# Both first products ahead of both transposes in the levels of a blockwise triangular inverse

## Chip, cores and metric

The kernel runs on one core of a Trainium2 chip. The metric is the device time of one execution in microseconds (us). The engines are called TensorE (PE in the profile), VectorE (DVE), ScalarE (ACT), GpSimd (POOL) and SyncE (SP).

## What is computed

A backbone of two layers over 512 latent tokens and 256 context tokens, 1024 channels wide, in float32. The change lies in layer 0, in the RWKV-7 part: 8 heads of 64 channels, each with a forward and a backward scan over the tokens.

```python
def update(S, w_t, k_t, v_t, a_t, b_t):
    sa = jnp.einsum('bhvk,bhk->bhv', S, a_t)
    return S * w_t[:, :, None, :] + sa[..., None] * b_t[:, :, None, :] + v_t[..., None] * k_t[:, :, None, :]
...
for d in range(2):
    rev = d == 1
    s_ctx, yc_d = rwkv_scan(state0, fc, d, need_ctx_out, rev)
    _, yl_d = rwkv_scan(s_ctx, fl, d, True, rev)
```

Attention, a gated convolution and two squared-ReLU MLPs make up the rest.

## The kernel before

The scan is done in 12 chunks of 64 tokens. Inside a chunk the effect of `sa` on later tokens is a unit lower triangular 64x64 system, which has to be inverted for every chunk, head and direction. The work goes over four pairs of heads (`for p in range(PAIRS)`, called pair 0 to 3 here). For each pair TensorE's program runs `chunk_matrices(p)` (the products of keys, decays and values), `inverse(p)` and `results(p)`.

`inverse(p)` refines an approximate inverse `X` in five levels, `lv` = 0 to 4, for two directions, `d` = 0 and 1, which do not depend on each other. One level of one direction is a ring over three engines:

- **First product** (`first_product`, L1011, 48 matmul records of 64x64): `LT` times `X`, into the two banks `2d` and `2d+1`. It waits for the sum of the level before (`x_ready`).
- **Mask** (`level_mask`, VectorE, L1379): the product, masked, to `W1` (`MT` in the profile).
- **Transposes** (`transposes`, L1024, 6 of 128x128): `X` of direction `d` to banks 4 and 5, three to each. Both directions use the same two banks, so the transposes of direction 1 wait, bank by bank, until ScalarE has copied those of direction 0 out (`xt_ready`).
- **Copies** (`inverse_rows`, ScalarE, L1250, one for each bank): to `XT`.
- **Second product** (`second_product`, L1038, in the last level L1041): needs the mask and both copies.
- **Sum** (`level_add`, VectorE, L1387): adds it to `X` (`xres` in the profile, since `X` and `LT` lie in that buffer). It releases the first product of the next level.

Other work of the neighbouring pairs is woven into TensorE's order by hand:

- `step(s)` (`state_step`, L1054): two per level, a product of the chunk-to-chunk recurrence of the pair before, of pairs 1 to 3 only. VectorE answers with two short instructions (L1395).
- `piece(i)` (`lora_piece`, L928): eight products for the decays and learning rates of the next pair, four in each of the levels 0 and 1, pairs 0 to 2 only. All go to bank 7, so piece `i` waits until ScalarE has taken the sigmoid of piece `i-1` out of it (`gate`, L1203).
- `bonus(p)` (L1085) in level 3.

ScalarE's and VectorE's orders are written out as well. In level 0 ScalarE does the copies of direction 0, loads a function table, does `gate` 0 and 1, then the copies of direction 1 and `gate` 2 and 3. In level 3 of the pairs 0 to 2 it does the copies of direction 0, a table load and two exponentials (L1209, L1211), and then the copies of direction 1. VectorE does mask 0, step, mask 1, sum 0, step, sum 1, with a scan (`cumulate`, L1311) in front of sum 0 in the levels 1 and 2 of the pairs 0 to 2, and another product (L1419) there in level 3. Meanwhile GpSimd multiplies and sums modulation weights (L890 to L896).

Of the kernel before, what the change touches and what calls it, by code (L numbers as in the profile page):

```python
# [61 lines left out]
def build(nc, A):  # L62
# [70 lines left out]
    def bank(i, lo=0, hi=512):  # L133
        return psum[i // 2][:, (i % 2) * 512 + lo:(i % 2) * 512 + hi]

    def K(name, lo=0, hi=None):
        a, n = cst_at[name]
        return cst[:, a + lo:a + (n if hi is None else hi)]
# [710 lines left out]
    def half(i):  # L849
        return slice(i * Q, (i + 1) * Q)  # L850

    def evacuated(p, i):

        kind = ORDER[i][0] in BY_ACT
        before = sum((k in BY_ACT) == kind for k, _ in ORDER[:i + 1])
        return (b_act, NACT * p + before) if kind else (b_dve, NDVE * p + before)
# [18 lines left out]
    with clear_then_block(S) as block:  # L875
# [44 lines left out]
        def _(pe):  # L920
# [82 lines left out]
            def first_product(p, lv, d):  # L1003

                pe.wait_ge(x_ready, 10 * p + 2 * lv + d + 1)
                if lv == 0:
                    pe.wait_ge(*evacuated(p, (18, 17)[d]))
                for g in range(GD):
                    for q in range(2):
                        for e in range(2):  # L1010
                            last = nc.tensor.matmul(bank(2 * d + e, g * Q, (g + 1) * Q)[half(q)], LT[half(e), d, g, q, :],  # L1011
                                                    X[half(e), d, g, q, :], start=True, stop=True)
                last.then_inc(s1_done, 1)

            def transposes(p, lv, d):

                n = 10 * p + 2 * lv + d
                for b in range(2):
                    if lv or d:
                        pe.wait_ge(xt_ready, 2 * (n - 1) + b + 1)  # L1020
                    else:
                        pe.wait_ge(*evacuated(p, 16))
                    for g in range(3 * b, 3 * b + 3):
                        last = nc.tensor.transpose(bank(4 + b, (g - 3 * b) * P, (g - 3 * b + 1) * P),  # L1024
                                                   X[:, d, g].rearrange("p q j -> p (q j)"), K("ident"))
                    last.then_inc(t_done, 1)
# [60 lines left out]
            def inverse(p):  # L1087

                def step(s):
                    if p:  # L1090
                        state_step(p - 1, s)

                def piece(i):
                    if p < PAIRS - 1:
                        lora_piece(p + 1, i)

                pe.wait_ge(*evacuated(p, 19))
                for lv in range(LVL):
                    first_product(p, lv, 0)
                    step(2 * lv + 1)  # L1100
                    transposes(p, lv, 0)
                    if lv < 2:
                        piece(4 * lv)
                    if lv == 3:
                        bonus(p)
                    first_product(p, lv, 1)
                    if lv < 2:
                        piece(4 * lv + 1)
                    transposes(p, lv, 1)
                    if lv < 2:  # L1110
                        piece(4 * lv + 2)
                    second_product(p, lv, 0)
                    step(2 * lv + 2)
                    if lv < 2:
                        piece(4 * lv + 3)
                    second_product(p, lv, 1)
# [941 lines left out]
```

## Time and profile before

| | us |
|---|---|
| three runs | 1876.32, 1867.37, 1876.82 |
| their median | 1876.32 |
| the profiled execution, its own time | 1864.56 |
| span of the profile in it | 1862.7 |
| TensorE busy | 1652.6 (89%) |
| the four inverses in the span | 435.7 to 707.1, in four parts |

The span is the time from the first to the last instruction in the profile. Lines in the profile are lines of the kernel before; a matmul row gives the instructions it merges and, in brackets, how long the engine stood still ahead of it and what ended that. "issue" means that no semaphore is seen to have ended it.

### The profile page before, as it was taken

The numbers are of one execution on the slowest core, as the hardware profiler recorded it, in microseconds if no ns is written. First come the engines' busy times: TensorE is split into PE (matmuls) and PEld (weight loads), VectorE is DVE, ScalarE is ACT, GpSimd is POOL, SyncE is SP. The second block draws the span as 40 slices with busy tenths as digits, with TensorE's granted clock in tenths as the row PEclk, the third lists the DMA queues.
The fourth block names the chain that finished last, engine by engine and source line by source line (L and its number), as shares of the span: only waits on it lengthen the run. The fifth ranks groups of instructions, "written<-read, shape, count | busy, mean of one in ns | idle before, by whom it ended". The sixth has DMA issues, their size and how long they took to land. (4 is left out here: it accounts for less than half of the span.)

```text
span 1862.7 us, 35286 instructions
## 1 busy us (share of the span) xinstructions
PE 1652.6 (89%) x15302; PEld 1294.3 (69%) x15302; DVE 799.7 (43%) x1083; ACT 578.4 (31%) x830; POOL 888.3 (48%) x352
## 2 busy tenths in 40 slices
PE   6699978958898887688999999989988799999995
PEld 2388847646777776364888888858867378888884
DVE  1421257666776763666211112680085821212125
ACT  2333235345353331414322223132221331323220
POOL 0443201039869580424778878843423434444442
PEclk9899989979999998798999999979999899999997
DMA  5341100003222131111443443311212112232221
GB/s 225 113 146 46 67 1 1 0 1 116 82 84 97 60 126 48 51 68 48 158 156 136 151 142 135 135 46 68 90 68 91 45 68 91 94 110 90 90 90 45
DMA packets 23449, 161.89 MB, mean 87 GB/s; under 512 B 2592, under 2 KB 3232, under 8 KB 4640
## 3 DMA queue, kind: packets, MB, share of 16 engines
q1 hardware_dynamic: 21744, 153.96, 23.3%
q10 hardware_dynamic: 1584, 6.13, 0.8%
q8 instruction: 100, 1.64, 0.4%
q14 instruction: 21, 0.17, 0.0%
HBM read 157.98 MB, written 2.10 MB: 86 GB/s over the span
## 5 line engine op out<-in xcount | busy, mean ns | idle before, releaser
L206 POOL TENSOR_TENSOR v<-raw,v 128x2048 fp32r<-128x2048 f32 x80 | 374.9, 4687 | 422.7 <-ACT v L195 348.6
L222 PE MATMUL bank<-hm,v 128*128 128x512 f32 x2304 | 538.8, 395 | 21.0 <-DVE hm L1758 10.0
L222 PEld LDWEIGHTS bank<-hm,v 128*128 128x128 f32 x2304 | 438.2, 191 | 122.3 <-issue 17.2
L222 PE MATMUL bank<-hid,v 128*128 128x512 f32 x1536 | 349.5, 389 | 0.0
L222 PEld LDWEIGHTS bank<-hid,v 128*128 128x128 f32 x1536 | 288.3, 188 | 59.9
L195 ACT ACTIVATE v<-raw 128x2048 fp32r<-128x2048 f32 x73 | 139.9, 1916 | 418.8 <-PE bank L222 418.8
L222 PE MATMUL bank<-h,w 128*128 128x512 f32 (+1 forms) x792 | 153.7, 357 | 14.2 <-POOL w L206 11.2
L1887 DVE TENSOR_TENSOR bank<-bank,rl 128x512 f32<-128x512 f32 x64 | 44.8, 700 | 275.9 <-ACT rl L1866 275.9
L222 PEld LDWEIGHTS bank<-h,w 128*128 128x128 f32 x792 | 129.8, 190 | 38.4 <-issue 13.4
L890 POOL TENSOR_TENSOR raw<-raw,cs 128x2048 f32<-128x2048 f32 x24 | 89.9, 3745 | 43.0 <-DVE at L1335 43.0
L1901 DVE TENSOR_TENSOR yb<-bank,yb 128x512 f32<-128x512 f32 x48 | 33.2, 692 | 170.8 <-PE bank L222 170.6
L894 POOL TENSOR_TENSOR raw<-raw 128x1024 f32<-128x1024 f32 (+1 forms) x48 | 95.9, 1998 | 3.8
L206 POOL TENSOR_TENSOR w<-raw,w 128x2048 fp32r<-128x2048 f32 x11 | 51.5, 4685 | 86.7 <-ACT w L195 86.7
L646 POOL TENSOR_TENSOR kk<-kk,knorm x32 | 12.4, 389 | 155.2 <-DVE knorm L785 155.2
L175 PE MATMUL bank<-cst 128*128 128x512 f32 x132 | 66.4, 651 | 7.7 <-PEq L1599 4.8
L1866 ACT ACTIVATE rl<-bank 128x512 f32<-128x512 f32 x64 | 37.6, 588 | 93.9 <-PE bank L222 74.1
L222 PE MATMUL bank<-ho,wo 128*128 128x512 f32 x192 | 50.1, 422 | 15.5 <-POOL ho L1566 11.0
L503 DVE TENSOR_TENSOR nb<-pad 128x770 f32<-128x770 f32 (+1 forms) x15 | 15.6, 1038 | 107.1 <-ACT pad L474 107.1
L206 POOL TENSOR_TENSOR wo<-raw,wo 128x2048 fp32r<-128x2048 f32 x4 | 19.4, 4849 | 83.9 <-ACT wo L195 83.9
L1585 DVE TENSOR_TENSOR ysq<-yb 128x512 f32<-128x512 f32 x28 | 45.4, 1622 | 32.3 <-ACT yb L1645 31.7
L1811 POOL TENSOR_TENSOR mprod<-mraw,cs 128x2048 f32<-128x2048 f32 x16 | 57.9, 3620 | 0.1
L222 PEld LDWEIGHTS bank<-ho,wo 128*128 128x128 f32 x192 | 38.7, 205 | 27.2 <-issue 13.0
(277 smaller groups left out, 2304.8 us busy)
## 6 DMA issues: line engine op xcount, KB each, us to landing
raw<-w_in SPq DMA_DIRECT2D x127, 1024.0 KB, 4.7
mraw<-wm_in SPq DMA_DIRECT2D x16, 1024.0 KB, 4.8
xres<-x_in ACTq DMA_DIRECT2D x1, 2048.0 KB, 9.3
xres<-x_in SPq DMA_DIRECT2D x1, 2048.0 KB, 9.1
out_T<-xres ACTq DMA_DIRECT2D x8, 256.0 KB, 2.0
kk<-ctx_in ACTq DMA_DIRECT2D x1, 1024.0 KB, 13.9
csa<-csa_in SPq DMA_DIRECT2D x1, 960.0 KB, 4.6
cst<-cst_in ACTq DMA_DIRECT2D x1, 864.0 KB, 17.3
```

The costliest lines, as they stand in the source:

```text
L175: nc.tensor.matmul(out[:, 0:width], K("ones"), cst[:, 0:width], start=True, stop=True)
L195: nc.scalar.activation(W[0][n % 2][:], raw[n % 2][:], ACT.Copy).then_inc(hi_ready[n % 2], 1)
L206: nc.gpsimd.tensor_tensor(W[1][n % 2][:], raw[n % 2][:], W[0][n % 2][:].bitcast(F32), SUB)\
L222: last = nc.tensor.matmul(bank(b(s, m), 0, hi - lo), W[w][s][:, k, m * P:(m + 1) * P], H[h][:, k, lo:hi], start=(k == 0 and w == h == 0), ...
L503: link(nc.vector.tensor_tensor(nb[:, a:N + 2], pad[j % 2][:, a:N + 2], pad[j % 2][:, a + 2:N + 4], ADD))
L890: nc.gpsimd.tensor_tensor(r[:], r[:], cs[:, :, 0].unsqueeze(2).to_broadcast([P, KT, 256]), MUL)\
L894: nc.gpsimd.tensor_tensor(r[:, 0:w, :], r[:, 0:w, :], r[:, w:2 * w, :], ADD).then_inc(mprod_ready, 1)
L1585: nc.vector.tensor_tensor(self.acc[:] if t == 0 else self.sq[:], y, y, MUL).then_inc(self.ready, 1)
L1811: nc.gpsimd.tensor_tensor(mprod[:], mraw[:], cs[:, :, 0].unsqueeze(2).to_broadcast([P, KT, 256]), MUL).then_inc(mprod_ready, 1)
L1866: nc.scalar.activation(rl[t % 2][:], bank(2 * (n % 2) + m), ACT.Relu)\
L1887: nc.vector.tensor_tensor(sq[t % 2], bank(2 * (n % 2) + m), rl[t % 2][:], MUL)\
L1901: i = nc.vector.tensor_tensor(yb[:, c, :], o, yb[:, c, :], ADD)
```

## The change

In each level TensorE now issues the first products of both directions ahead of the transposes of both. The pieces stay in their order, each behind a transposing group: piece 0 behind the first, 1 and 2 both behind the second. The lines of VectorE, ScalarE, GpSimd and SyncE are the same, and so is every instruction and every bank.

```diff
@@ -1098,16 +1098,15 @@
                 for lv in range(LVL):
                     first_product(p, lv, 0)
                     step(2 * lv + 1)
+                    first_product(p, lv, 1)
                     transposes(p, lv, 0)
                     if lv < 2:
                         piece(4 * lv)
                     if lv == 3:
                         bonus(p)
-                    first_product(p, lv, 1)
+                    transposes(p, lv, 1)
                     if lv < 2:
                         piece(4 * lv + 1)
-                    transposes(p, lv, 1)
-                    if lv < 2:
                         piece(4 * lv + 2)
                     second_product(p, lv, 0)
                     step(2 * lv + 2)
```

TensorE's program in pair 1, level 0, before. L1011 is a first product, L1054 a step, L1024 the transposes of one direction, L928 a piece, L1038 a second product; one listed instruction is two matmul records in the profile, where the operands are float32:

```order
L1011 MATMUL bank<-xres 64x64 x24
L1054 MATMUL bank<-kk 64x64 x4
L1024 MATMUL bank<-cst,xres 128x128 x6
L928 MATMUL bank<-lora,lw 128x256
L1011 MATMUL bank<-xres 64x64 x24
L928 MATMUL bank<-lora,lw 128x256
L1024 MATMUL bank<-cst,xres 128x128 x6
L928 MATMUL bank<-lora,lw 128x512
L1038 MATMUL bank<-MT,XT 64x64 x24
L1054 MATMUL bank<-Z,kk 64x64 x4
L928 MATMUL bank<-lora,lw 128x512
L1038 MATMUL bank<-MT,XT 64x64 x24
```

The same place after the change:

```order
L1011 MATMUL bank<-xres 64x64 x24
L1054 MATMUL bank<-kk 64x64 x4
L1011 MATMUL bank<-xres 64x64 x24
L1024 MATMUL bank<-cst,xres 128x128 x6
L928 MATMUL bank<-lora,lw 128x256
L1024 MATMUL bank<-cst,xres 128x128 x6
L928 MATMUL bank<-lora,lw 128x256
L928 MATMUL bank<-lora,lw 128x512
L1038 MATMUL bank<-MT,XT 64x64 x24
L1054 MATMUL bank<-Z,kk 64x64 x4
L928 MATMUL bank<-lora,lw 128x512
L1038 MATMUL bank<-MT,XT 64x64 x24
```

The first product of direction 1 has moved ahead of the first transposes; the second transposes now stand ahead of the second piece, so that the second and third piece are neighbours.

TensorE in pair 1, level 3, before, from its first product on:

```order
L1011 MATMUL bank<-xres 64x64 x24
L1054 MATMUL bank<-Z,kk 64x64 x4
L1024 MATMUL bank<-cst,xres 128x128 x6
L1085 MATMUL bank<-bs,cst 128x512
L1011 MATMUL bank<-xres 64x64 x24
L1024 MATMUL bank<-cst,xres 128x128 x6
L1038 MATMUL bank<-MT,XT 64x64 x24
L1054 MATMUL bank<-Z,kk 64x64 x4
L1038 MATMUL bank<-MT,XT 64x64 x24
```

And after the change:

```order
L1011 MATMUL bank<-xres 64x64 x24
L1054 MATMUL bank<-Z,kk 64x64 x4
L1011 MATMUL bank<-xres 64x64 x24
L1024 MATMUL bank<-cst,xres 128x128 x6
L1085 MATMUL bank<-bs,cst 128x512
L1024 MATMUL bank<-cst,xres 128x128 x6
L1038 MATMUL bank<-MT,XT 64x64 x24
L1054 MATMUL bank<-Z,kk 64x64 x4
L1038 MATMUL bank<-MT,XT 64x64 x24
```

Here the transposes of direction 0 stand behind the first product of direction 1. In the levels 2 and 4 nothing is left between the two groups of transposes, as the listing after the change shows with twelve in a row:

```order
L1011 MATMUL bank<-xres 64x64 x24
L1054 MATMUL bank<-Z,kk 64x64 x4
L1011 MATMUL bank<-xres 64x64 x24
L1024 MATMUL bank<-cst,xres 128x128 x12
L1038 MATMUL bank<-MT,XT 64x64 x24
L1054 MATMUL bank<-Z,kk 64x64 x4
L1038 MATMUL bank<-MT,XT 64x64 x24
```

## Rows read from the trace of the kernel before

**Rows 1.** the page, busy time of TensorE: busy us, share of the span, instructions

```profile
PE 1652.6 (89%) x15302; PEld 1294.3 (69%) x15302; DVE 799.7 (43%) x1083; ACT 578.4 (31%) x830; POOL 888.3 (48%) x352
```

**Rows 2.** one 40 us stretch: busy us of each engine, TensorE's granted clock, DMA share, GB/s

```profile
520.00:560.00 40.00, 37.37 (x1180) 31.28 (x1176) 31.71 (x47) 19.13 (x34) 22.39 (x14) 1.00 0.21 76
```

**Rows 3.** TensorE in time order, pair 0, level 0: start us, duration us, line, tiles

```profile
435.66 0.93 PE L1011 MATMUL bank<-xres 64*64 64x64 f32 x48 [0.90 <-ACT k_tok L1242]
436.52 0.87 PE L1024 MATMUL bank<-cst,xres 128*128 128x128 f32 x6
...
439.82 0.70 PE L928 MATMUL bank<-lora,lw 64*128 64x256 f32 x2 [0.94 <-ACT at L1203]
440.44 0.88 PE L1024 MATMUL bank<-cst,xres 128*128 128x128 f32 x6
...
444.21 0.93 PE L1038 MATMUL bank<-MT,XT 64*64 64x64 f32 x48
444.96 0.88 PE L1011 MATMUL bank<-xres 64*64 64x64 f32 x48
```

**Rows 4.** ScalarE in time order, pair 0, level 0

```profile
437.10 0.87 ACT L1250 ACTIVATE XT<-bank 128x384 f32<-128x384 f32 x2 [1.49 <-PE bank L1024]
437.99 1.28 ACT L1203 ACT_TABLE_LOAD   x1
439.29 0.47 ACT L1203 ACTIVATE at<-bank,prm 128x256 f32<-128x256 f32 x1
440.55 0.47 ACT L1203 ACTIVATE at<-bank,prm 128x256 f32<-128x256 f32 x1 [0.79 <-PE bank L928]
```

**Rows 5.** VectorE in time order, the add behind pair 0's level 0

```profile
445.21 0.95 DVE L1387 TENSOR_TENSOR xres<-xres,bank 128x768 f32<-128x768 f32 x1 [0.96 <-PE bank L1038]
```

**Rows 6.** VectorE in time order, end of pair 1's level 2

```profile
537.70 0.93 DVE L1387 TENSOR_TENSOR xres<-xres,bank 128x768 f32<-128x768 f32 x1
```

**Rows 7.** TensorE in time order, pair 1, level 3

```profile
538.68 0.93 PE L1011 MATMUL bank<-xres 64*64 64x64 f32 x48 [0.99 <-DVE xres L1387]
539.43 0.41 PE L1054 MATMUL bank<-Z,kk 64*64 64x64 f32 x8
539.77 0.87 PE L1024 MATMUL bank<-cst,xres 128*128 128x128 f32 x6
...
545.02 0.93 PE L1038 MATMUL bank<-MT,XT 64*64 64x64 f32 x48 [0.76 <-ACT XT L1250]
```

**Rows 8.** ScalarE in time order, pair 1, level 3

```profile
540.36 0.87 ACT L1250 ACTIVATE XT<-bank 128x384 f32<-128x384 f32 x2 [2.32 <-PE bank L1024]
541.25 1.28 ACT L1209 ACT_TABLE_LOAD   x1
...
544.02 0.86 ACT L1250 ACTIVATE XT<-bank 128x384 f32<-128x384 f32 x2
```

**Rows 9.** all engines in time order, GpSimd and a scan of pair 2

```profile
603.40 3.61 POOL L890 TENSOR_TENSOR raw<-raw,cs 128x2048 f32<-128x2048 f32 x1
...
604.55 4.07 DVE L1311 TENSOR_TENSOR_SCAN at<-cst,at 128x768 f32<-128x768 f32 x1
```

**Rows 10.** the waits from 430 to 720 us: us in total, times, longest

```profile
PE bank L1011 <- DVE xres L1387: 3.3, 4, 1.0
...
PE bank L1011 <- issue: 3.1, 5, 1.3
...
PE bank L928 <- ACT at L1203: 2.3, 3, 0.9
...
PE bank L1054 <- issue: 2.1, 2, 1.2
...
PE bank L1085 <- issue: 1.9, 1, 1.9
PE bank L1038 <- issue: 1.9, 3, 1.0
PE bank L1038 <- ACT XT L1250: 1.8, 2, 1.0
```

## The prediction

> **What bounds the kernel now.** I read the page first, then the windows, then TensorE's timeline through one inverse, and beside it those of ScalarE and VectorE. TensorE is busy for 89% of the span [rows 1]. In the 40 us that hold most of pair 1's inverse it works 37.4, VectorE 31.7, GpSimd 22.4 and ScalarE 19.1, at a granted clock of 1.00, the full 2.4 GHz [rows 2]. So TensorE's own order sets the end of an inverse. The reader should see in rows 3 that one group starts where the last leaves off; what remains are short stops. Rows 10 give those of the stage: for semaphores 3.3 us (a first product behind VectorE's sum), 2.3 us (a piece behind the sigmoid of the piece before) and 1.8 us (a second product behind ScalarE's copies), 7.4 us in all. Another 9.0 us are "issue", which no semaphore ended (3.1 + 2.1 + 1.9 + 1.9).
>
> Delays inside an inverse reach the end of the kernel, I assume one to one: `results` and the next pair follow on the same in-order engine, the output projection needs their sums, and the reload of x waits for the last of them.
>
> **Spacings that I use.** First product to transposes 0.86 us (435.66 to 436.52), transposes to the next group 0.81 (440.44 to 441.25, read as 0.80), a second product to a first one 0.75 [rows 3]. A step ahead of transposes is 0.34 [rows 7]; ahead of 64x64 products I take 0.25, shorter by the same 0.1 as 0.75 is than 0.86 (estimate). Transposes to the start of their copies 0.58; a piece to its sigmoid 0.73, sigmoid 0.47, and 0.06 to the next piece (439.76 to 439.82) [rows 3, 4]. Second product to the start of its sum 1.00, sum 0.95 [rows 3, 5], and 0.05 to the first product (538.63 to 538.68) [rows 6, 7]. Both copies take 0.87, one of them half of that and a little overlap, about 0.48 [rows 4].
>
> **The parts of the change.**
>
> *The same instructions, fewer switches.* Nothing is added. First product to first product costs 0.75 instead of 0.86, so each level saves 0.11 us.
>
> *A. A new wait for the sum of direction 1 (levels 1 to 4).* The first product of direction 1 needs the sum that its second product began: 1.00 + 0.95 + 0.05 = 2.00 us after that product's start. Before, the first product, step and transposes of direction 0 lay in between. Now only the first product and, in the pairs 1 to 3, the step do: TensorE is there after 0.75 + 0.75 = 1.50 us in pair 0 and 1.75 in the others, and stands still for 0.50 and 0.25. Queued behind it are the transposes of direction 0, which would be ready, and ScalarE waits for them.
>
> *B. Transposes back to back (levels 2 and 4, in pair 3 also 0 and 1).* Banks 4 and 5 have to be copied out first. The first half is free at 0.58 + 0.48 + 0.06 = 1.12 us, TensorE is there at 0.80: 0.32 us, which the first product of direction 1 used to cover.
>
> *C. The pieces in level 0 (pairs 0 to 2).* The transposes come 0.75 later (0.86 less 0.11), and with them copies, table load, sigmoid and so the second piece, which TensorE already waits 0.94 for [rows 3]. From second to third piece it was 1.43 (439.82 to 441.25) with transposes inside; now it is 0.73 + 0.47 + 0.06 = 1.26 with nothing inside. Net 0.75 - 0.17 = +0.58.
>
> *D. The pieces in level 1 (pairs 0 to 2).* No wait before. Now the third piece waits 1.26 - 0.63 = 0.63 for the sigmoid. With A, less 0.11: +1.02 in pair 0, +0.77 in 1 and 2.
>
> *E. Level 2 (pairs 0 to 2): the gain.* VectorE's scan stands between mask 1 and sum 0, and the first product of level 3 waits 0.99 for that sum [rows 7]. An earlier first product of direction 1 brings mask 1 and the scan forward by 0.65 us (0.36 in pair 0). TensorE's own way then decides: 1.25 to that product, then 0.86 + 1.12 + 0.80 and 2.00 to the sum of direction 0, 6.03 against 6.44 us (6.20 in pair 0), that is -0.41 and -0.17.
>
> *F. Level 3 (pairs 0 to 2).* ScalarE does copies 0, a table load, two exponentials and only then copies 1 [rows 8]; from the start of transposes 0 to the second product of direction 1 this chain takes 5.25 us and ends 0.76 us after TensorE got there [rows 7]. The chain begins 0.86 - 0.11 + 0.25 (wait A), about 1.0 us later, and everything behind it too: +1.0.
>
> *G. Level 4.* A and B less 0.11: +0.71 in pair 0, +0.46 in the others.
>
> *H. Pair 3* has no pieces, scans or exponentials: +0.21 in level 0, +0.46 in each of 1, 2 and 4, and +0.15 in level 3, where the bonus parts the transposes. Sum 1.74.
>
> Pair 0: 0.58 + 1.02 - 0.17 + 1.00 + 0.71 = 3.14. Pair 1: 0.58 + 0.77 - 0.41 + 1.00 + 0.46 = 2.40. Pair 2 the same, less one thing: its scan in level 1 took 4.07 us, because a GpSimd instruction with SBUF inputs was under way until 607.01; the scan ended 1.6 us after that [rows 9], and I estimate that the next first product stood 0.4 us for it. In the longer level this is covered: 2.0. With pair 3 the sum is 3.14 + 2.40 + 2.00 + 1.74 = **+9.3 us**. As a test, the same spacings in the old order give 9.20 us from the first product of pair 0 to that of its level 1, where rows 3 have 9.30.
>
> A rule of the Trainium skill bears on the scan: "SBUF — State Buffer", section "Who interferes with whom", says that a VectorE instruction with two SBUF inputs contends with GpSimd's reads, and one with at most one doesn't. The trace agrees for the scan (4.07 us beside GpSimd), and the sums, with one input in PSUM, hold at 0.95. By this rule masks and sums may move freely and only scans can meet GpSimd at a worse moment: up to 2.5 us (607.01 less 604.55), which the pieces would cover in level 1.
>
> *Against it: stops that change their cause.* While TensorE waits for a semaphore, its instructions go on arriving, so an "issue" stop behind a new wait shrinks. The bound is that each of the 9.0 us is absorbed up to the delay that its inverse has by then, which by the places of the stops is 1.2, 0.6, 2.2 and 1.8 us for the four pairs, 5.8 at most; the other bound is nothing. I take 1.5, nearer to nothing, since what TensorE consumes later it also asks for later. The sum becomes 9.3 - 1.5 = **+7.8 us**.
>
> *Costed at nothing:* GpSimd's modulation and key products, since TensorE arrives later so their slack grows; without it TensorE would stand still in `results`. SyncE's loads hang on GpSimd alone.
>
> **Forecast.** The profiled execution took 1864.56 us, so it would take 1872.4. The median of the three runs is 11.8 us above it, and I place the change on that median: 1876.3 + 7.8 = **1884 us**.
>
> **Rivals.**
>
> 1. *Nothing is absorbed*: +9.3 to +11, 1886 to 1887. For it: the stops may hang on when instructions arrive, which nothing ties to TensorE's waits. It would also be so if wait A is longer because VectorE's step instructions push sum 1 back. Against it: 5.0 us of the stops stand ahead of first products and the bonus [rows 10], which come behind new waits.
> 2. *The stops swallow most of it*: 9.3 - 5.8 = +3.5, 1880. For it: 9.0 us of issue stops are as much as the whole sum. Against: the 2.1 us ahead of steps (L1054) come early in their inverse, where there is little delay yet [rows 10].
> 3. *Faster*: the earlier first product of direction 1 lets VectorE mask early, so that all 7.4 us of semaphore waits vanish [rows 10], 1869 on the median. It decides if sum 1 is done by the time that TensorE has issued the first product of direction 0, that is if the 2.00 us above is really under 1.5. Rows 3 and 5 speak against it, and the level 3 chain on ScalarE starts later whatever VectorE does.
> 4. *The clock falls*: waits that are longer, up to 1.7 us in level 3, let the granted clock fall to 1.2 GHz for about a level. A level is 6.3 us (538.68 to 545.02) [rows 7], so one fall costs up to that: +14, 1890. Against it: the clock stayed at 1.00 around stops of 0.99 us [rows 2, 7]. [...]
> 5. *The change does nothing*, as TensorE isn't the bound: within 1 us. I fold it into the second.
>
> **Chances.** Forecast 0.48, nothing absorbed 0.24, swallowed 0.14, faster 0.07, clock 0.07. A measurement of this kernel can tell about 0.5%, 9.4 us. Slower by more than that: the clock (0.07), most of the first rival (0.20) and a fifth of the forecast (0.10), 0.37. Faster by more: 0.05, since even all of the third rival gives 7.4 us. Within: 0.58. The range goes from 1870 (the second rival in a draw of runs as low as the lowest before, 9 us under the median) to 1893 (the clock rival and a little).
>
> **What would show it.** In the profile after, each inverse of the pairs 0 to 2 should be 2 to 3 us longer and that of pair 3 about 1.7. Waits of L1011 for L1387 should double in number at 0.25 to 0.5 us each; new waits of L1024 for L1250 of 0.3 us; L928 waiting for L1203 also with its third piece, 0.63; L1038 in level 3 waiting 1.7 for L1250 instead of 0.76; and the wait of level 3's first product should fall from 0.99 to 0.25. I am wrong if the transposes don't wait for the copies, if sum 1 is early, or if the delay of an inverse doesn't appear at the end of the stage.

## The result, and the profile after

The changed kernel took 1890.71 us (median of 9 runs, 1882.81 to 1896.22), the kernel before on the same chip 1874.43 (9 runs, 1865.4 to 1879.48). The ratio is 1.0104 [1.0078, 1.013]: slower, by 19.5 us if the ratio is taken of 1874.43; the two medians lie 16.3 us apart, the means 17.4. The forecast was +7.8. The time itself lies inside the forecast's range of 1870 to 1893, whose upper end was set by the rival of the clock.

The profiled execution took 1894.38 us against 1864.56 before. Of the 29.9 us between their spans 25.2 lie in the four inverses, taken from the first L1011 of a pair to the end of its last sum (L1386; L1387 before): they add up to 184.6 us against 159.4. The three stretches between them, where TensorE prepares the next pair, grew from 112.0 to 117.2, and the rest of the kernel by −0.5.

The busy times on the page answer to [rows 1]. TensorE does the same 15302 products in 9.7 us more of busy time, which can't be a wait.

```profile
PE 1662.3 (88%) x15302; PEld 1300.7 (69%) x15302; DVE 796.2 (42%) x1083; ACT 577.8 (31%) x830; POOL 887.2 (47%) x352
```

TensorE in time order, pair 0, level 0; this answers to [rows 3].

```profile
434.38 1.63 PE L1011 MATMUL bank<-xres 64*64 64x64 f32 x96 [0.90 <-ACT k_tok L1241]
435.94 0.87 PE L1024 MATMUL bank<-cst,xres 128*128 128x128 f32 x6
436.74 0.70 PE L928 MATMUL bank<-lora,lw 64*128 64x256 f32 x2
437.37 0.88 PE L1024 MATMUL bank<-cst,xres 128*128 128x128 f32 x6
439.23 0.70 PE L928 MATMUL bank<-lora,lw 64*128 64x256 f32 x2 [0.99 <-ACT at L1202]
440.49 2.07 PE L928 MATMUL bank<-lora,lw 64*128 64x512 f32 x2 [0.56 <-ACT at L1202]
442.49 1.56 PE L1038 MATMUL bank<-MT,XT 64*64 64x64 f32 x48
443.98 2.07 PE L928 MATMUL bank<-lora,lw 64*128 64x512 f32 x2
445.98 1.56 PE L1038 MATMUL bank<-MT,XT 64*64 64x64 f32 x48
447.31 2.86 PE L1011 MATMUL bank<-xres 64*64 64x64 f32 x96
```

The reader should see three things. The 96 products of both directions stand in front, as the diff says. The second piece waits 0.99 where it waited 0.94, the third 0.56 where it waited for nothing. And the third piece, 2 products of 512 columns, takes 2.07 us. In the trace of before, the same two products take 1.12; from here on each product is slower: the last row has the same 96 products as the first and takes 2.86 us instead of 1.63. The windows of this stretch say why: the last column but two is the granted clock.

```profile
434.00:440.00 6.00, 4.56 (x112) 3.35 (x112) 1.82 (x2) 2.99 (x6) 5.76 (x4) 1.00 0.39 158
440.00:444.00 4.00, 3.51 (x51) 1.89 (x51) 0.00 (x0) 1.89 (x4) 4.00 (x2) 0.54 0.53 178
444.00:448.00 4.00, 4.00 (x82) 2.50 (x82) 1.35 (x2) 0.69 (x1) 3.84 (x3) 0.50 0.22 88
448.00:452.00 4.00, 4.00 (x90) 3.38 (x83) 3.28 (x4) 1.03 (x3) 3.92 (x3) 0.68 0.55 164
452.00:456.00 4.00, 3.44 (x59) 2.05 (x58) 2.20 (x2) 2.24 (x5) 3.92 (x2) 1.00 0.25 102
```

From about 440.3 us until 450.6 the clock is at half, 1.2 GHz; added up over windows of 2 us that makes 10.2 us. The same windows of the trace of before all read 1.00; one of them, for comparison:

```profile
444.00:448.00 4.00, 4.00 (x148) 3.20 (x148) 2.07 (x3) 2.04 (x4) 3.92 (x2) 1.00 0.54 221
```

The same happens in pair 1. Behind its pieces it reads:

```profile
525.00:528.00 3.00, 2.44 (x4) 0.68 (x4) 0.00 (x0) 1.24 (x3) 2.84 (x3) 0.61 0.27 112
528.00:531.00 3.00, 3.00 (x58) 2.29 (x58) 1.22 (x3) 0.69 (x1) 2.92 (x3) 0.50 0.18 27
531.00:534.00 3.00, 3.00 (x74) 1.94 (x76) 0.43 (x2) 0.69 (x1) 2.92 (x2) 0.50 0.81 328
534.00:537.00 3.00, 3.00 (x98) 2.84 (x90) 2.57 (x5) 0.15 (x1) 2.92 (x2) 0.68 0.02 5
```

In level 3 of pair 1, ScalarE's copies come late, as they should by term F. It answers to [rows 7], where the wait was 0.76.

```profile
557.15 0.41 PE L1054 MATMUL bank<-Z,kk 64*64 64x64 f32 x8
559.33 0.93 PE L1038 MATMUL bank<-MT,XT 64*64 64x64 f32 x48 [1.77 <-ACT XT L1249]
560.05 0.91 PE L1011 MATMUL bank<-xres 64*64 64x64 f32 x48
```

And here is a stop that has no semaphore, in pair 3, in front of the last seven records of the second product of direction 1 in level 1. From here on F0 and F1 are short for the first products of the two directions, S0 and S1 for the second ones:

```profile
708.52 0.81 PE L1038 MATMUL bank<-MT,XT 64*64 64x64 f32 x39
713.42 0.38 PE L1038 MATMUL bank<-MT,XT 64*64 64x64 f32 x4 [4.10 <-issue]
...
713.69 1.40 PE L1011 MATMUL bank<-xres 64*64 64x64 f32 x44
```

The waits from 430 to 740 us answer to [rows 10]: us in total, times, longest.

```profile
PE bank L959 <- issue: 6.7, 7, 1.8
...
PE bank L1038 <- issue: 5.6, 2, 4.1
PE bank L1038 <- ACT XT L1249: 5.5, 3, 2.0
...
PE bank L928 <- ACT at L1202: 4.7, 6, 1.0
...
PE bank L1011 <- issue: 4.1, 6, 1.3
...
PE bank L1024 <- ACT XT L1249: 2.5, 10, 0.3
...
PE bank L1011 <- DVE xres L1386: 1.9, 3, 1.1
PE bank L928 <- ACT bt L1202: 1.7, 3, 0.6
```

L928 now waits 9 times instead of 3, L1024 ten times at 0.25, L1038 for the copies 5.5 us instead of 1.8. The sum in front of L1011 shrank from 3.3 to 1.9. Most of this is what the prediction asked for; only the waits for that sum, which should have doubled in number, went from four to three, and the inverses, which should have grown by 2 to 3 us, grew by 6.2, 7.7, 6.8 and 4.4. What the prediction didn't expect is the clock, and that the "issue" stops did not shrink.

**The bookkeeping of one trace.** I took from each trace the length of each inverse, the time in it at half clock (over windows of 2 us: one less the clock, twice, times the length), and the "issue" stops of TensorE in it; then the same stops in the stretches between, up to pair 3. By pair, us:

```
                    length of the inverses        at half clock         issue stops           between: length, issue
before              39.7  40.9  42.5  36.4        0    0    0    0      1.2  0.9  2.3  4.5    112.0   13.4
changed             45.9  48.6  49.3  40.8        10.2 10.2 10.2 3.4    0    2.0  2.1  6.3    117.2   18.7
```

From each length I take its issue stops, and from the changed one also the waits forecast (3.14, 2.40, 2.00, 1.74). Pair 0, which has no stop after the change: 45.88 − (39.66 − 1.2) − 3.14 = 4.3 us. Pairs 1 to 3 in the same way: 4.2, 5.0 and 0.8. These 14.4 us are what is left for 34.0 us at half clock. So the +25.2 of the inverses can be read as 9.3 of waits as forecast, 1.5 more of issue stops and 14.4 of clock; the last is a remainder and not measured by itself.

### The profile page after: what moved, and what is told of

Same layout as the page of the kernel before. It is cut to its first block and busy times, and to the rows that moved or that the text cites. A ratio compares the mean times of both kernels' runs of the same rounds, so it can differ in the third digit from the quotient of the medians.

```text
span 1892.6 us, 35286 instructions
## 1 busy us (share of the span) xinstructions
PE 1662.3 (88%) x15302; PEld 1300.7 (69%) x15302; DVE 796.2 (42%) x1083; ACT 577.8 (31%) x830; POOL 887.2 (47%) x352
## 5 line engine op out<-in xcount | busy, mean ns | idle before, releaser
L222 PEld LDWEIGHTS bank<-hm,v 128*128 128x128 f32 x2304 | 437.9, 191 | 123.1 <-issue 17.2
L222 PE MATMUL bank<-h,w 128*128 128x512 f32 (+1 forms) x792 | 155.1, 359 | 14.6 <-POOL w L206 11.3
L1900 DVE TENSOR_TENSOR yb<-bank,yb 128x512 f32<-128x512 f32 x48 | 33.2, 692 | 177.0 <-PE bank L222 176.8
L503 DVE TENSOR_TENSOR nb<-pad 128x770 f32<-128x770 f32 (+1 forms) x15 | 15.6, 1038 | 107.1 <-ACT pad L474 107.1
L1249 ACT ACTIVATE XT<-bank 128x384 f32<-128x384 f32 x80 | 34.9, 488 | 76.4 <-PE bank L1024 76.4
```

What stands on the lines that cost most here:

```text
L222: last = nc.tensor.matmul(bank(b(s, m), 0, hi - lo), W[w][s][:, k, m * P:(m + 1) * P], H[h][:, k, lo:hi], start=(k == 0 and w == h == 0), ...
L503: link(nc.vector.tensor_tensor(nb[:, a:N + 2], pad[j % 2][:, a:N + 2], pad[j % 2][:, a + 2:N + 4], ADD))
L1249: nc.scalar.activation(XT[:, d, 3 * b:3 * b + 3].rearrange("p g e j -> p (g e j)"), bank(4 + b, 0, 384), ACT.Copy).then_inc(xt_ready, 1)
L1900: i = nc.vector.tensor_tensor(yb[:, c, :], o, yb[:, c, :], ADD)
```

## The experiments

**Are the falls of the clock due to the waits at the pieces?** `filler` gives TensorE a product of its own at the two places where it would stand, on a constant, into a bank that is free, behind a semaphore long passed. Nothing else differs from the changed kernel.

```diff
+            def filler(p, n):
+                pe.wait_ge(w_ready, 10 * p + 1)
+                nc.tensor.matmul(bank(0, 0, n), K("ones"), cst[:, 0:n], ...)
...
                     transposes(p, lv, 1)
                     if lv < 2:
+                        if lv == 0 and p < PAIRS - 1:
+                            filler(p, 512)
                         piece(4 * lv + 1)
+                        if lv == 0 and p < PAIRS - 1:
+                            filler(p, 256)
                         piece(4 * lv + 2)
```

> The changed kernel plus six products of the ones matrix whose result nobody reads: in level 0 of the pairs 0 to 2 one of 512 columns ahead of the second piece and one of 256 ahead of the third, in the waits of 0.99 and 0.56 us that the trace after has there. Clock theory: these two waits let the granted clock fall to 1.2 GHz in the three pairs; with the waits filled it stays at 1.00 in level 0 and 1, the inverse of pair 0 takes about 41.6 us (38.4 before without its stops, and 3.1 of waits) instead of 45.9, and the kernel gains some 13 us on the changed one, ratio to before 1.003 to 1.005. Rival, the order itself or TensorE's lighter work in level 0 lets the clock fall, not the waits: nothing gained, ratio 1.01.

Measured: 1881.11 us, ratio 1.0051 [1.0022, 1.008], against 1871.99 for the kernel before in the same comparison. Half of the loss is gone though the pieces start as late as in the changed kernel, a little less than the 13 us expected. TensorE's rows of pair 0:

```profile
438.14 1.02 PE L1090 MATMUL bank<-cst 128*128 128x512 f32 x2
439.30 0.70 PE L928 MATMUL bank<-lora,lw 64*128 64x256 f32 x2
439.92 0.70 PE L1090 MATMUL bank<-cst 128*128 128x256 f32 x2
440.56 1.12 PE L928 MATMUL bank<-lora,lw 64*128 64x512 f32 x2
441.61 0.93 PE L1038 MATMUL bank<-MT,XT 64*64 64x64 f32 x48
```

L1090 is the filler. The third piece starts at 440.56, in the changed kernel at 440.49, and takes 1.12 us instead of 2.07. None of pairs 0, 1 and 3 spends time at half clock, pair 2 has 3.4 us of it. And pair 0 less its stops is 44.43 − 2.6 = 41.8 us, where the forecast of its waits gives 38.46 + 3.14 = 41.6. Pair 1 has 42.7 (forecast 42.4), pair 3 33.2 (33.6). The terms of the sum hold in this trace.

**Which levels cost what?** Three kernels take the new order in a part of the levels: `new = lv == 0`, `new = lv > 0` and `new = lv > 1` in

```diff
+                    new = lv > 1
...
-                    first_product(p, lv, 1)
+                    if new:
+                        first_product(p, lv, 1)
                     transposes(p, lv, 0)
```

and so on with the lines behind.

> The new order in level 0 alone, levels 1 to 4 as before. Clock theory: the clock falls in the pairs 0 to 2 as in the changed kernel, since both waits are there; 3 times 4.3 us for the clock and 2.0 us of waits, +15 us, ratio 1.008. Rival, each level brings its own share in equal parts: about a fifth of the 20 us, +4, ratio 1.002.

> The new order in the levels 1 to 4, level 0 as before. Clock theory: no fall in the inverses of the pairs 0 to 2; only the forecast waits without those of level 0, 9.3 - 2.0 = +7.3 us, ratio 1.004. Rival, equal parts: four fifths of 20, +16, ratio 1.008.

> The new order in the levels 2 to 4 only. Clock theory: no fall; waits by the forecast's terms E, F, G and H: 1.5 + 1.1 + 1.1 + 1.1 = +4.8 us, ratio 1.0025, with the waits at the first product of level 3 down from 0.99 to about 0.25 us and at its second product of direction 1 up from 0.76 to 1.7. Rival, equal parts: +12, ratio 1.006.

Measured: level 0 alone 1880.76 us, ratio 1.0048 [1.0027, 1.0069], 9.0 us; levels 1 to 4 1883.5, 1.0083 [1.0056, 1.011], 15.6 us; levels 2 to 4 1879.9, 1.0039 [1.0019, 1.006], 7.3 us. Level 0 costs less than I had expected and levels 1 to 4 twice as much. The two together give 1.0131 against 1.0104 for the whole, which by their intervals is no difference. The levels 2 to 4 alone agree with what I had expected (1.0025) as well as with the rival (1.006); their trace has no half clock within an inverse, and the waits are there: 2.00, 1.70 and 1.77 us at the second product of direction 1 in level 3, and none above 0.36 for a sum. In the trace of level 0 alone the pairs 0 to 2 spend 13.7, 10.2 and 10.2 us at half clock: the new order in level 0 is enough for falls in each pair. In that of levels 1 to 4 pair 1 has none and measures 41.87 us with no stops, where its forecast is 39.99 + 1.82 = 41.8. The waits are right here too; beside them this trace has 6.8 us at half clock in its inverses, 13.6 between them, and stops of 17.0 us between them. The waits alone don't explain these, and why they are there wasn't tested.

**Does the kernel before have the falls as well?** Its first trace had none within an inverse. Two more were taken, and a second one of the changed kernel.

> The kernel before, unchanged, for a second trace of it. Clock theory: no stretch at 1.2 GHz inside the four inverses and their sum within 3 us of 159.4, the differences being stops without a semaphore. Rival, the first trace of before was a lucky one and such falls belong to every kernel here: the clock is low for 3 us or more inside at least two of the inverses.

> The kernel before once more, unchanged, for a third trace. Theory: the new order makes falls of the clock inside the inverses more frequent, it does not create them; before shows 0 and 17 us at 1.2 GHz in its two traces, so here between 0 and 17, under the 34 us of the changed kernel. Rival: both orders have the same falls and the first trace of each was chance, then 30 us or more.

> The changed kernel once more, unchanged, for a second trace. Theory: 20 to 34 us at 1.2 GHz inside the inverses, the waits as in its first trace (0.99 and 0.56 us in level 0, 0.25 at the second transposes, 2.0 and 1.7 in level 3). Rival, as above: 10 us or less.

```
                    length of the inverses        at half clock         issue stops           between: length, issue
before, second      39.5  44.8  43.7  36.4        0    10.2 6.8  0      1.0  1.3  1.8  3.9    113.7   12.9
before, third       43.8  42.6  42.7  36.7        3.4  3.4  3.0  0      0    2.3  2.4  4.2    117.8   16.9
changed, second     46.5  45.1  47.4  41.1        13.6 6.8  6.8  3.4    0    0    1.4  6.5    118.3   17.2
```

They took 1871.13, 1879.82 and 1888.54 us. The kernel before does lose its clock, and at the very wait that I had held up as harmless; what I expected of its second trace, no half clock within an inverse, was wrong. Its second trace, TensorE in pair 1:

```profile
516.09 0.70 PE L928 MATMUL bank<-lora,lw 64*128 64x256 f32 x2 [0.94 <-ACT at L1203]
516.71 1.49 PE L1024 MATMUL bank<-cst,xres 128*128 128x128 f32 x6
518.13 2.07 PE L928 MATMUL bank<-lora,lw 64*128 64x512 f32 x2
```

Six transposes take 1.49 us instead of 0.88 right behind the wait of 0.94, and the piece 2.07. So the same wait that left the clock at 1.00 in [rows 2, 3] takes it away in another execution. The three traces of before spend 0, 17.0 and 9.8 us of their inverses at half clock, those of the changed kernel 34.0 and 30.6. The new order makes frequent what was there. And the third trace of before is 15.3 us longer than the first with the same program. A part of this is a long wait in pair 0, behind a scan that GpSimd's work ran beside; in the first trace that scan took 1.75 us and the wait was 0.88:

```profile
460.32 5.07 DVE L1311 TENSOR_TENSOR_SCAN at<-cst,at 128x768 f32<-128x768 f32 x1
466.29 0.95 PE L1011 MATMUL bank<-xres 64*64 64x64 f32 x36 [4.45 <-DVE xres L1387]
```

**Is it the two waits together?** One theory was that it takes both. `filler` ahead of the third piece alone leaves the 0.99.

> The changed kernel with only the second wait of level 0 filled (256 columns ahead of the third piece), so that the wait of 0.99 us ahead of the second piece stands alone, as in the kernel before. Two-waits theory: the clock stays at 1.00 in the levels 0 and 1 of the pairs 0 to 2, time as with both filled, ratio 1.005. Rival, the longer wait alone does it in this order: three falls of about 10 us at 1.2 GHz, ratio 1.010.

The opposite: a one-column sigmoid ahead of the level's first copies has ScalarE load that table early, when it isn't waited for, which takes away the 0.99 and leaves the 0.56.

```diff
+                    if lv == 0 and p < PAIRS - 1:
+                        nc.scalar.activation(small[:, 40:41], small[:, 0:1], ACT.Sigmoid)
                     inverse_rows(p, lv, 0)
```

> The changed kernel with one sigmoid of a single column ahead of ScalarE's first copies of level 0, in the pairs 0 to 2, whose result nobody reads: the function table is then loaded while ScalarE waits for the transposes. Chain theory: the wait ahead of the second piece (0.99 us) goes, that ahead of the third (0.56) stays, the clock doesn't fall, 3 times 0.99 us and 3 times 4.3 us are gained, ratio to before 1.003. Rival, the table load isn't what the piece waits for: the wait stays at 0.99 and the clock falls as in the changed kernel.

> The changed kernel with both tables loaded early and a product of 256 columns of the ones matrix ahead of the third and the seventh piece. What is left of the forecast's waits is 9.3 - 3 x 0.99 - 3 x 1.28 = 2.5 us. Theory: ratio to before 1.000 to 1.002, at most 10 us at 1.2 GHz inside the inverses. Rival, something else in the new order costs time: ratio 1.005 or more as in the run with both waits of level 0 filled.

Measured: 1890.42 us, 1.0113 [1.0078, 1.0147] for the first; 1889.74, 1.009 [1.0053, 1.0127] for the second, where I expected 1.003; 1882.34, 1.0076 [1.0045, 1.0108] for the third, which has both tables early (the exponentials' too) and a filler ahead of the third piece in the levels 0 and 1. None of the three came as the theory had it: the first took the time of the rival, the third should have come to 1.002 at most. The theory that one wait alone leaves the clock at full fell. With 0.99 alone, pair 0 and pair 2 lose 13.6 and 10.2 us to half clock, pair 1 none and pair 3 3.4. With 0.56 alone the clock holds through level 0, and falls in level 1:

```profile
437.39 0.70 PE L928 MATMUL bank<-lora,lw 64*128 64x256 f32 x2
438.65 1.12 PE L928 MATMUL bank<-lora,lw 64*128 64x512 f32 x2 [0.56 <-ACT at L1202]
...
440.56 1.12 PE L928 MATMUL bank<-lora,lw 64*128 64x512 f32 x2
...
443.61 0.93 PE L1011 MATMUL bank<-xres 64*64 64x64 f32 x48 [0.38 <-DVE xres L1388]
444.47 0.55 PE L1024 MATMUL bank<-cst,xres 128*128 128x128 f32 x3
446.58 0.80 PE L1024 MATMUL bank<-cst,xres 128*128 128x128 f32 x3 [1.57 <-issue]
447.31 1.22 PE L928 MATMUL bank<-lora,lw 64*128 64x256 f32 x2
```

The piece at 437.39 has no wait any more, those at 438.65 and 440.56 take 1.12: the clock is full. Behind the sum (0.38) and a stop of 1.57 that no semaphore ended, three transposes take 0.80 and a piece 1.22 instead of 0.70. In the third kernel it is the same place, with 0.38 and 1.51, although no piece waits in its level 0; its pairs 1 to 3 have no half clock. So the clock doesn't hang on one wait, and not every fall begins at the pieces.

**All traces counted.** Every trace has three pairs with pieces. The table counts in how many the clock fell at those of level 0, that is, from the start of the second piece to 1.5 us after the start of the third:

```
what waits in level 0                        pairs   falls there
both pieces, 0.99 and 0.56 us                 12        11
one piece, 0.45 to 0.99 or 0.56 us            24         4
neither (fillers or early table)              21         0
```

The 12 are those of the changed kernel (two traces), of level 0 alone and of the changed kernel with small loads (below). Of the four falls with one wait two are in the second trace of before, two in the kernel with 0.99 alone; one more pair was at half clock already. So the two waits together bring the fall nearly every time, one alone now and then, and with none there was no fall at this place, in either order. That is what the waits at the pieces do. It doesn't cover the falls in later levels, as the one above: the late fall of the third kernel and that of 10.2 us in pair 0 of the old order with tables early and scan late (below) both begin right behind a stop (1.51 and 1.44 us) that no semaphore ended.

**The table loads in the kernel before.** The same trick without the change, and once with the scan behind the next sum, so that level 3's first product needn't wait (term E's 0.99).

> The kernel before with one early sigmoid as above, and one early exponential of a single column ahead of ScalarE's first copies of level 3. Chain theory: the waits of 0.94 us at the second piece and of 1.0 and 0.76 us at the second product of direction 1 in level 3 go; 4 to 5 us in all, ratio 0.9975, this is the version that might beat both. Rival, those waits turn into stops without a semaphore: ratio 1.000.

> The kernel before with both tables loaded early, and VectorE's scans of the levels 1 and 2 behind the sum of direction 1 instead of ahead of the sum of direction 0. The waits of about 1 us at the first product of level 3 (3.3 us in all in the first trace of before) should go, the next mask of direction 0 has 1.5 us to spare for it. Theory: 7 to 8 us less than before, ratio 0.996. Rival, the late scan holds up the next masks and second products: ratio as with early tables alone, 0.998, or above.

```diff
-                    if p < PAIRS - 1 and lv in (1, 2):
-                        cumulate(p + 1, lv - 1)
...
+                    if p < PAIRS - 1 and lv in (1, 2):
+                        cumulate(p + 1, lv - 1)
```

Measured: 1866.89 us, ratio 0.9981 [0.9955, 1.0007], and 1869.49, 0.9991 [0.9963, 1.0018]. Neither can be told from the kernel before; the second should have come to 0.996. In the first trace the waits at L928 and at L1038 for copies are gone and the inverses add up to 156.3 us, against 159.4 to 165.8. In the second, L1011 waits 0.9 us for sums instead of 3.3, but L1038 waits 2.8 for masks, 2.4 of it once in pair 0, behind a late scan of 3.99 us, and that pair has 13.7 us at half clock. In the pairs 1 and 2 the wait for a mask is 0.2 us each.

**Where do the issue stops come from?** One theory was that TensorE's instructions arrive late while SyncE loads the modulation's weights (a DMA share of up to 0.81 in the windows above). Here those loads bring only 256 of their 2048 columns from the third block on (so the modulation values are not the reference's), in the kernel before, in the changed one, and in the changed one with `filler`.

```diff
-                sp_next(sp, n)
+                if n + 2 < S_OUT:
+                    ...
+                    sp.dma_start(raw[n % 2][:].rearrange("p k m -> p (k m)")[:, 0:256], A["w"][n + 2][:, 0:256])
+                else:
+                    sp_next(sp, n)
```

> The kernel before with 22 of the 24 weight loads that SyncE starts during this stage cut to an eighth (256 of 2048 columns), so its modulation values are not the reference's; all engines' instructions are the same. Theory: the stops come from instructions queued behind these loads, so the 22 us of them (8.6 in the inverses and 14.4 between) fall under 8, and the kernel takes 10 to 18 us less, ratio to before 0.990 to 0.995. Rival, the stops belong to TensorE's instruction supply by itself: stops and time unchanged.

> The changed kernel with the same loads cut to an eighth, modulation values again not the reference's. Theory: without the stops there are fewer falls of the clock; this run lies 9.3 us of waits above the kernel before with small loads, plus up to 13 if the three falls in level 0 stay. Rival, falls need a stop as well as the waits: then no falls, and 9 us above.

> The changed kernel with both waits of level 0 filled and the same loads cut to an eighth, modulation values again not the reference's. Theory: no falls in the inverses, few stops; 9.3 us above the kernel before with small loads, the inverses 41.6, 42.4, 42.4 and 33.6 us long. Rival: something in the new order that is neither wait, clock nor stop, then 14 us or more above.

```
                       length of the inverses        at half clock        issue stops          between: length, issue
f1 before              38.5  40.6  40.3  32.9        0    0    0    0     0    0    0.2  1.4   114.0   12.1
f2 changed             41.5  45.1  47.7  37.3        0    6.8  6.8  0     0    0    2.0  4.0   112.1   13.7
f3 changed, filled     42.8  43.2  45.1  35.3        3.4  0    0    0     0    0.7  2.0  2.4   109.9   12.9
```

Measured: 1860.42 us, 0.9951 [0.9923, 0.9979]; 1880.4, 1.0045 [1.0022, 1.0068]; 1873.0, 0.9998 [0.9976, 1.002]. The loads are a part of it: in the kernel before, the stops inside the inverses go from 8.6 us (mean of three traces) to 1.6 in one trace, and the kernel is 9 us faster, a little less than the 10 to 18 expected. Between the inverses they go only from 14.4 to 12.1, so the 23.0 us of both fall to 13.7 and not under 8. Changed against before is +20.0 us even with small loads, and +12.6 with the fillers, between the 9.3 of the theory and the 14 of its rival. Pair 0 of f2, with no half clock and no stop, against that of f1 is the cleanest reading of the waits that I have: 41.48 − 38.52 = 2.96 us, forecast 3.14.

With small loads the changed order keeps stops of 6.0 and 5.1 us where the kernel before has 1.6. The other theory was that they come in long unbroken runs of 64x64 products, 48 records in 0.75 us, and that the new order makes these longer: where nothing is woven in, S0, S1, F0 and F1 now follow each other with 192 records. (The stop of 4.10 us above is in S1, where the run up to it is the same in both orders.) One product of 512 columns between the second and the first products should let the instructions catch up:

```diff
                     second_product(p, lv, 1)
+                    if lv < LVL - 1:
+                        nc.tensor.matmul(bank(4), K("ones"), cst[:, 0:512], ...)
```

> The changed kernel with waits filled and small weight loads (modulation values not the reference's), plus one product of 512 columns of the ones matrix between the last second product of a level and the first product of the next, 16 in all, each 0.96 us for two records. It is not meant to be faster. Supply theory: instructions catch up during these, the stops inside the inverses fall from 5.1 us to 2 or less. Rival: the stops have nothing to do with the length of the runs, 4 us or more stay.

> The changed kernel with waits filled and small weight loads once more, a second trace (modulation values not the reference's): if the stops are a property of the order, again 4 to 6 us of them inside the inverses, most in the pairs 2 and 3; if chance, under 2.

Measured: 1877.91 us and 1871.54. The stops in the inverses are 1.9 us with the spacer, in one trace, and 5.1 and 6.8 without, in two. That fits the theory, but between the inverses, where no spacer stands, they are 8.3 against 12.9 and 14.6, so a part of the difference comes from elsewhere. As a way to gain time it is nothing: the execution with the sixteen added products took 6.4 us more than the one without.

**Where the stops stand.** Their places say more than their lengths. Count TensorE's matmul records from the start of the kernel. The 459 issue stops of all nineteen traces between 430 and 740 us stand at only 49 places (to within one record), and these lie on one grid, about 127.4 records apart: from one to the next it is 126 to 128 records or a multiple of that. At the records 3856, 6148 and 8440 every trace stops. The order of the instructions doesn't move the grid, and added instructions are counted in it. Record 9585 of the kernel, in pair 3, is where the 4.10 us stand: in both orders it has 41 records of its S1 ahead of it. In the kernel with 0.99 alone three fillers, six records, stand ahead, and the stop comes six records earlier in S1:

```profile
709.03 0.44 PE L1038 MATMUL bank<-MT,XT 64*64 64x64 f32 x11 [4.14 <-issue]
```

So an issue stop belongs to the stream of instructions, which reaches TensorE in blocks of that many products, and not to what the instruction does or waits for. The loads and the order change only how long the next block keeps it waiting. Why this one block came 4.1 us late in the four traces with the new order in level 1 and large loads that show it, and 0.4 to 1.0 us late in the old order, isn't shown.

## Why the prediction was wrong

**The terms of the waits were right in the main.** A, the sum of direction 1: 0.38 and 0.36 in pair 0 where I had 0.50; in the other pairs it doesn't show, forecast 0.25. B, the banks: 0.25, ten times, where I had 0.32. C and D, the pieces: 0.99 and 0.56 in level 0 and 0.56 in level 1, forecast 0.63 for each of the latter. F, level 3: 2.00 in pair 0 (1.00 before, in the row that answers to it) and 1.77 in pair 1 (0.76), forecast 1.0 more; in pair 2 it is 1.77 where the first trace of before had none, since a stop of 1.94 us ahead of the bonus hid it. E, the gain, is true in pair 1, where no product of level 3 waits for the sum any more in either trace of the changed kernel; in pair 0 it varies, 1.14, 0.67 and 0.34 us in three traces of the new order against 0.88. H: pair 3 of the filled kernel 33.2 us, forecast 33.6. The best check of all together, without falls and stops, is 2.96 for 3.14 in pair 0.

**The step that failed is the clock, which the sum put at nothing and the fourth rival at a chance of 0.07.** The reason stands there as "Against it: the clock stayed at 1.00 around stops of 0.99 us". The observation was true and worth little: it was one execution, and in the next one of the same kernel the clock fell behind just such a stop of 0.94. The rival also had the place wrong: it looked to the waits of up to 1.7 us in level 3, behind which only one fall began in the two traces of the changed kernel (3.4 us, in pair 0 of the second). The falls came at the pieces of level 0, at 0.99 and 0.56 us, one in each of three pairs, 6.8 to 10.2 us long. And it priced one fall at 6.3 us (538.68 to 545.02 isn't a whole level, as the second product of direction 1 is still to come); that its 1890 is near the measured 1890.71 is luck. Filling both waits brought the ratio from 1.0104 to 1.0051, about 10 us. The Trainium skill, "TensorE: Matmul & The Clock Gate", section "HAM oscillation — how this bites in real kernels", tells of a kernel whose clock fell each time at waits for DMA of about 3 to 5 us between bursts of matmuls. The waits that did it here are much shorter, so that section doesn't give this case; the traces do.

**The second step that failed is the absorption, −1.5.** The stops inside the inverses were not absorbed: 10.4 and 7.9 us in two traces against 8.9, 8.0 and 8.9. Those between the inverses, which I hadn't costed, are 18.7 and 17.2 against 13.4, 12.9 and 16.9, a mean of 3.5 us more. The first rival named the reason, "the stops may hang on when instructions arrive", and the fixed places of the stops show it: a stop waits for the next block of instructions, whatever TensorE stood for before.

**The sum once more.** Mean of the traces, changed less before: inverses 182.4 − 163.3 = 19.1 us, of which 9.3 are forecast waits, 0.6 stops and 9.2 what is left for 23.4 us more at half clock; between them 117.8 − 114.5 = 3.3, as much as the stops there. That is 22.4; the mean spans differ by 19.6, so the head and the tail are 2.8 shorter; the measured ratio gives 19.5. What came is the first rival (nothing absorbed) and the fourth together, and about 3 us more of stops between the inverses that no rival had.

**The same sum from all executions.** The 9.2 us are too much for the clock as a whole: in the traces the changed kernel has 23.4 us more of half clock in its inverses, but 7 us less in the rest of the kernel, where the instructions are the same. Each recorded execution has its span and its mean granted clock, which give its time at half clock over the whole kernel, 2 x (1 − clock) x span. The 93 executions of the kernel before that were taken beside the experiments have 208.6 us of it in the mean and take 1871.1 us; those with more are longer, by 0.35 us for each us (standard error 0.03; a correlation of 0.79, not an experiment). The nine of the changed kernel have 224.5 us. With this price, the forecast waits that each kernel keeps, and the stops of its traces in and between the inverses less the mean 23.0 us of before, an estimate can be set beside each measured mean. In us, against the kernel before:

```
                                waits   clock   stops    sum   measured (standard error)
changed                          9.3     5.6     4.1    19.0    19.2 (1.6)
both waits filled                9.3     1.0     0.5    10.8    10.4 (1.4)
0.99 alone                       9.3     4.6     4.6    18.5    19.8 (2.0)
0.56 alone                       6.3     6.6     6.3    19.2    17.6 (1.6)
all waits treated                2.5     4.3     4.6    11.4    10.7 (1.5)
new in level 0                   2.0     7.5    -1.7     7.8    10.1 (1.4)
new in levels 1 to 4             7.3     1.4     4.1    12.8    14.1 (1.9)
new in levels 2 to 4             4.8     0.6     5.6    11.0     8.1 (1.4)
before, small loads              0      -1.3    -9.2   -10.5    -9.4 (1.7)
changed, small loads             9.3     3.9    -3.6     9.6     9.6 (1.5)
changed, filled, small loads     9.3     0.5    -5.0     4.8     1.6 (0.9)
```

Every line agrees within 3.2 us, though the stops come from one trace each (two of the changed kernel, three of before). So the changed kernel is 9.3 us slower by its waits, about 5.6 by the clock and about 4 by stops. The prediction had the first, put the second at nothing and the third at −1.5.

**What stays open.** Why a single wait at the pieces brings a fall in one pair and not in the next wasn't settled, nor what starts the falls of the later levels. The kernel with all waits treated keeps 1.0076 with one fall of 13.7 us in pair 0 and stops of 11.4 in its inverses: taking the waits away doesn't take these away. Why the stops grow by 4 us with the new order is open as well. And executions of one program differ by up to 24 us (30 of the kernel before, 1862.63 to 1886.84), of which half clock and stops are only a part. No version beats the kernel before beyond doubt: the early tables give 0.9981 with 1 inside the interval.

## What to carry to other kernels

Two orders of the same instructions on the bounding engine differ by what the other engines' chains need first: here ScalarE's copies and sigmoids hang on the transposes, and everything put in front of these is paid again at the pieces and in level 3. A short wait has two prices, its length and the clock: ask for each new wait whether another stands near it, and fill both with products that nobody needs before judging the order by them. "The clock stayed at full" is a statement on one execution; take three traces before a chance of 0.07 rests on it. Stops without a semaphore are worth counting by instruction number before a cause is sought in what the instructions do.

## What the runs showed of the hardware

- The clock fell to half behind a wait of 0.99 us followed by one of 0.56, with TensorE at work in between, and stayed there for 10.2 us, through windows in which TensorE was busy throughout. I had not expected that of waits that short. At this place it fell in 11 of 12 pairs with both waits, in 4 of 24 with one and in none of 21 with neither. In three traces of one kernel the inverses had 0, 17.0 and 9.8 us at half clock.
- TensorE stopped 4.10 us in the midst of a run of 64x64 products with nothing to wait for, and in front of the same record, number 9585, in three more traces: of the changed kernel again 4.10, with level 0 old 4.10, with the filler at the second wait 4.14 us. With the sigmoid's table early it was 2.46, with small loads 1.36, and with both fillers there was none there; in three traces of the kernel before it was 0.98, 0.70 and 0.43 us. All 459 such stops of the stage in nineteen traces lie on a grid of about 127.4 matmul records, in either order: TensorE is kept waiting by its own instructions, block by block. With the loads beside it cut to an eighth, the stops in the inverses of the kernel before went from 8.6 to 1.6 us.
- A table load of 1.28 us on ScalarE could be taken off the path by one activation on a single column, ahead of the copies: the piece's wait of 0.99 was gone. It didn't make the kernel measurably faster.
